# Later heads' queries and keys of the stick-breaking mixer from seven quarter products, their weight sums made by GpSimd

## The reference, cut to what matters

```python
def stick_breaking_mixer(x, w_in, w_out):
    q, k, v = jnp.split(x @ w_in, 3, axis=-1)            # 1024 columns each
    heads = lambda a: a.reshape(B, S, SB_HEADS, HEAD_DIM) # 16 heads of 64
    return stick_breaking_attention(heads(q), heads(k), heads(v)) @ w_out

def one_block(b):                                         # stick_breaking_attention
    z = jnp.einsum('bqhd,bshd->bhqs', qb, k) * scale
    log_1m = jnp.where(mask, jax.nn.log_sigmoid(-z), 0.0)
    between = lax.cumsum(log_1m, axis=3, reverse=True) - log_1m
    w = jnp.where(mask, jnp.exp(jax.nn.log_sigmoid(z) + between), 0.0)
    return jnp.einsum('bhqs,bshd->bqhd', w, v)
```

## Time and profile before

| What | us |
|---|---|
| Median of 3 runs (1143.28 to 1144.44) | 1143.73 |
| The profiled execution | 1144.65 |
| Its span in the trace | 1142.9 |
| PE busy, of the span | 1058.1 |
| DVE busy | 401.9 |
| ACT busy | 221.1 |
| POOL busy (6 instructions) | 1.0 |

### The profile page before, as it was taken

The page is one execution under the profiler, slowest core; times in us unless marked ns, Lnnn a source line. Parts: engine busy times, 40 slices in busy tenths (PEclk is TensorE's granted clock), DMA queues, the critical chain, the costliest instruction groups (busy, mean ns, idle before and its releaser), DMA issues.

```text
span 1142.9 us, 15878 instructions
## 1 busy us (share of the span) xinstructions
PE 1058.1 (93%) x6490; PEld 527.8 (46%) x6490; DVE 401.9 (35%) x1070; ACT 221.1 (19%) x509; POOL 1.0 (0%) x6
## 2 busy tenths in 40 slices
PE   9999999999999999999999999987878897789996
PEld 6555455554786455554655544423222332224231
DVE  5776463114556654114736734101100010001003
ACT  2045341111024432111131522101000000001011
POOL 0000000000000000000000000000000000000000
PEclk9999999999999999999999999999988999899999
DMA  9878478977943378996836738999999999999995
GB/s 320 185 199 292 174 266 357 421 329 251 339 163 132 122 275 346 421 381 208 322 130 228 290 136 290 386 430 425 428 429 426 428 430 427 428 430 428 399 424 231
DMA packets 84997, 363.66 MB, mean 318 GB/s; under 512 B 23138, under 2 KB 28612, under 8 KB 61892
## 3 DMA queue, kind: packets, MB, share of 16 engines
q1 hardware_dynamic: 84132, 362.59, 81.3%
q10 hardware_dynamic: 800, 0.17, 0.1%
HBM read 361.69 MB, written 1.05 MB: 317 GB/s over the span
## 4 chain that ended last, share of the span: by engine, by line
PE 67%; DMA 23%; DVE 6%; ACT 1%; issue 1%; SPq 1%; DVEq 0%
DMA weights<-in_expert_w_down_dram 16%; PE bank L1471 13%; PE bank L1025 6%; PE bank L1003 6%; PE bank L1535 5%; PE bank L1583 5%; DMA weights<-in_expert_w_up_dram 4%; PE bank L1515 4%; PE bank L1684 3%; PE bank L1015 2%; PE bank L1812 2%; PE bank L1403 2%; PE bank L1957 2%; PE bank L1242 2%; DMA weights<-in_expert_w_gate_dram 1%; PE bank L1917 1%
## 5 line engine op out<-in xcount | busy, mean ns | idle before, releaser
L1471 PE MATMUL bank<-weights,mixed 128*32 128x512 f32 x992 | 226.3, 610 | 31.3 <-DMA weights<-in_expert_w_gate_dram 17.9
L1471 PEld LDWEIGHTS bank<-weights,mixed 128*32 128x32 f32 x992 | 63.1, 112 | 181.1 <-issue 169.6
L1025 PE MATMUL bank<-weights,mixed 128*128 128x512 f32 x192 | 89.8, 602 | 0.0
L1003 PE MATMUL bank<-weights,x_transposed 128*128 128x512 f32 x192 | 89.2, 601 | 0.0
L1535 PE MATMUL bank<-weights,work 128*32 128x512 f32 x464 | 62.1, 670 | 25.5 <-DMA weights<-in_expert_w_down_dram 21.0
L3098 DVE TENSOR_TENSOR work<-work,bank 64x512 f32<-64x512 f32 (+1 forms) x22 | 15.0, 682 | 157.7 <-PE bank L1471 156.0
L2285 ACT ACTIVATE work<-bank 128x512 f32<-128x512 f32 (+1 forms) x32 | 19.0, 594 | 229.5 <-PE bank L1535 190.7
L3000 DVE COPY work<-bank 64x512 f32<-64x512 f32 (+1 forms) x30 | 20.7, 690 | 117.0 <-PE bank L1535 75.1
L1684 PE MATMUL bank<-work,heads_transposed 128*128 128x512 f32 x120 | 56.0, 607 | 4.6 <-ACT work L2285 4.6
L1471 PE MATMUL bank<-weights,projected 128*64 128x256 f32 x512 | 57.0, 381 | 0.0
L3005 DVE COPY work<-bank 128x256 f32<-128x256 f32 (+1 forms) x22 | 10.8, 493 | 127.4 <-PE bank L1487 127.4
(11 more groups left out here) (464 smaller groups left out, 1405.8 us busy)
## 6 DMA issues: line engine op xcount, KB each, us to landing
weights<-in_expert_w_gate_dram SPq DMA_DIRECT2D x28, 2048.0 KB, 16.9
weights<-in_expert_w_up_dram SPq DMA_DIRECT2D x28, 2048.0 KB, 17.7
weights<-in_expert_w_down_dram SPq DMA_DIRECT2D x24, 2048.0 KB, 19.1
weights<-in_moe_w_down_dram SPq DMA_DIRECT2D x16, 2048.0 KB, 14.7
weights<-in_moe_w_gate_dram SPq DMA_DIRECT2D x14, 2048.0 KB, 13.0
weights<-in_moe_w_up_dram SPq DMA_DIRECT2D x12, 2048.0 KB, 15.2
weights<-in_sb_w_in_dram SPq DMA_DIRECT2D x6, 2048.0 KB, 19.5
weights<-in_w_in_dram SPq DMA_DIRECT2D x6, 2048.0 KB, 16.2
```

Of the source, the lines that this page charges most:

```text
L1003: i = mm(BANK[bank or 6 + t][:, :], XT[:, kt, t * P:(t + 1) * P], w[:, kt, :], start=kt == 0, stop=kt == KT - 1)
L1025: i = mm(BANK[bank][:, :], mixT[:, kt, t * P:(t + 1) * P], w[:, kt, :], start=kt == 0, stop=kt == KT - 1)
L1471: i = mm(b[n_slots * c:n_slots * (c + 1), e * F:(e + 1) * F], x[:, kt, q * n_slots:(q + 1) * n_slots], extra_weights(c, kt) if outside els ...
```

## The change

Chunks 3 and 4 are no longer projected by eight half-pieces but by seven products (`second`, 16 matmuls of 128 columns each), with the same scheme as the first heads, as fillers of steps 0 to 6. The fillers of chunk 5 move from steps 8, 9 to 7, 8; step 9 has none. GpSimd makes the four sums of weights (`VS1` to `VS4`, 128x2048 each, written into quarters of the chunks' own slots that are no longer read). DVE adds the products up (`sb_sums`, in steps 3, 5, 6 and 7), ACT copies three of them (`sb_copies`, steps 1, 2 and 4). The copy of the last values moves on ACT from step 11 to step 12. The sums of inputs `XS` are kept in `norm_params` instead of `heads_transposed`, and so the load of the second layer's normalisation rows moves from ahead of the mixer's output weights to behind the third chunk of the following experts.

```diff
+        XS = [quarter(NORM_[:, CH * i:CH * (i + 1)]) for i in range(4)]
+        VS1, VS2, VS3, VS4 = K1_HI, Q1_LO, K1_LO, Q1_HI
...
@@ block.gpsimd
+            pool.wait_ge(half_psum, 4)
+            nc.gpsimd.tensor_tensor(VS1, K1_LO, K1_HI, ALU.add).then_inc(pool_filled, 1)
+            pool.wait_ge(half_psum, 5)
+            pool.wait_ge(pool_filled, 2)
+            nc.gpsimd.tensor_tensor(VS3, Q1_LO, K1_LO, ALU.subtract).then_inc(pool_filled, 1)
+            pool.wait_ge(pool_filled, 3)
+            nc.gpsimd.tensor_tensor(VS2, VS1, Q1_LO, ALU.subtract).then_inc(pool_filled, 1)
+            pool.wait_ge(products_psum, AB_PRODUCTS + 3)
+            pool.wait_ge(pool_filled, 4)
+            nc.gpsimd.tensor_tensor(VS4, Q1_HI, VS2, ALU.subtract).then_inc(pool_filled, 1)
@@ block.tensor
-                         (N_SB + 5, 0): (half_copied, 5), (N_SB + 5, 1): (proj_copied, 11)}
+                         (N_SB + 5, 0): (proj_copied, 11), (N_SB + 5, 1): (sums_ready, AB_SUMS + 6)}
...
+            def second_4():
+                second(6, K1_HI, XS[3]).then_inc(half_psum, 1)
+            def second_1():
+                second(7, Q1_LO, lo[:, :, 0:P]).then_inc(half_psum, 1)
+            def second_2():
+                pe.wait_ge(half_copied, 4)
+                second(6, Q1_HI, hi[:, :, 0:P]).then_inc(products_psum, 1)
+            def second_5():
+                pe.wait_ge(half_copied, 5)
+                pe.wait_ge(pool_filled, 2)
+                second(7, VS1, XS[0]).then_inc(products_psum, 1)
+            def second_6():
+                pe.wait_ge(sums_ready, AB_SUMS + 4)
+                pe.wait_ge(pool_filled, 4)
+                second(6, VS2, XS[1]).then_inc(products_psum, 1)
+            def second_7():
+                pe.wait_ge(proj_copied, 10)
+                second(7, VS3, XS[2]).then_inc(products_psum, 1)
+            def second_3():
+                pe.wait_ge(sums_ready, AB_SUMS + 5)
+                pe.wait_ge(pool_filled, 5)
+                second(6, VS4, hi[:, :, P:S]).then_inc(chunk_done, 2)
             sb_filler = {
-                0: lambda: project_half_T(N_SB + 3, 0, 0, 8), 1: lambda: project_half_T(N_SB + 3, 0, 8, 16),
...
-                8: lambda: project_half(N_SB + 5, 0, 0, 4), 9: lambda: project_half(N_SB + 5, 0, 4, 8),
+                0: second_4, 1: second_1, 2: second_2, 3: second_5, 4: second_6, 5: second_7, 6: second_3,
+                7: lambda: project_half(N_SB + 5, 0, 0, 4), 8: lambda: project_half(N_SB + 5, 0, 4, 8),
@@ block.scalar
-            sb_copies = {2: (3, 0), 4: (3, 1), 6: (4, 0), 8: (4, 1), 10: (5, 0), 11: (5, 1)}
+            sb_copies = {1: copy_4, 2: copy_1, 4: copy_5, 10: lambda: take_sb_half(0), 12: lambda: take_sb_half(1)}
@@ block.vector
+            def after_second_2():
+                dve.wait_ge(half_copied, 5)
+                dve.wait_ge(products_psum, AB_PRODUCTS + 3)
+                tt(second_q[:, :, 0:P], four(U2), four(BANK[6]), ALU.add).then_inc(sums_ready, 1)
+            def after_second_6():
+                link(tt(U2, U2, BANK[6], ALU.add))
+                tt(second_q[:, :, P:S], second_q[:, :, P:S], four(U2), ALU.add).then_inc(sums_ready, 1)
+            def after_second_7():
+                link(tt(U2, U2, BANK[7], ALU.add))
+                tt(second_k[:, :, P:S], second_k[:, :, P:S], four(U2), ALU.add)
+                tt(second_k[:, :, 0:P], second_k[:, :, 0:P], four(U2), ALU.add).then_inc(sums_ready, 1)
+            def after_second_3():
+                dve.wait_ge(chunk_done, N_SB + 5)
+                tt(second_q[:, :, P:S], second_q[:, :, P:S], four(BANK[6]), ALU.add).then_inc(proj_copied, 1)
+            sb_sums = {3: after_second_2, 5: after_second_6, 6: after_second_7, 7: after_second_3}
             for s in range(16 + 5):
...
+                if s in sb_sums:
+                    sb_sums[s]()
```

More of the change, by code:

```diff
@@ L142 @@
 OUT_DMAS = 3
-SB_SUMS = 7
-SB_PRODUCTS = 7
+SB_SUMS = 10
+SB_PRODUCTS = 11
 AB_SUMS = 4
@@ L509, in build @@
         WS1, WS2, WS3, WS4 = WK[:, 0:HALF_SLOT], WK[:, HALF_SLOT:SLOT], K_LO, Q_HI
-        XS = [quarter(QK[:, 1024 + CH * i:1024 + CH * (i + 1)]) for i in range(4)]
+        XS = [quarter(NORM_[:, CH * i:CH * (i + 1)]) for i in range(4)]
+        Q1_LO, Q1_HI = (slot(N_SB + 3)[:, at:at + HALF_SLOT] for at in (0, HALF_SLOT))
+        K1_LO, K1_HI = (slot(N_SB + 4)[:, at:at + HALF_SLOT] for at in (0, HALF_SLOT))
+        VS1, VS2, VS3, VS4 = K1_HI, Q1_LO, K1_LO, Q1_HI
         U3, U4, U2 = QK[:, 0:CH], QK[:, CH:2 * CH], QK[:, 6 * CH:7 * CH]
@@ L778, in moe @@
                         load_unit_chunk(0, j)
+                        if L == 1 and j == 2:
+                            load_norm(2, (a["ln_mix_g"][1], a["ln_mix_b"][1]))
                     sp.wait_ge(roped, 7)
@@ L1877, in sb_out_first, with second @@
                     out_part(N_SB + 6, 0, t, 6 + t, range(kt, kt + 1))
-            sb_filler = {
-                0: lambda: project_half_T(N_SB + 3, 0, 0, 8), 1: lambda: project_half_T(N_SB + 3, 0, 8, 16),
-                2: lambda: project_half_T(N_SB + 3, 1, 0, 8), 3: lambda: project_half_T(N_SB + 3, 1, 8, 16),
-                4: lambda: project_half_T(N_SB + 4, 0, 0, 8), 5: lambda: project_half_T(N_SB + 4, 0, 8, 16),
-                6: lambda: project_half_T(N_SB + 4, 1, 0, 8), 7: lambda: project_half_T(N_SB + 4, 1, 8, 16),
-                8: lambda: project_half(N_SB + 5, 0, 0, 4), 9: lambda: project_half(N_SB + 5, 0, 4, 8),
+            def second(bank, weights, x):
+                w = quarter(weights)
+                for c in range(4):
+                    for kt in range(KT // 2):
+                        i = mm(BANK[bank][:, c * P:(c + 1) * P], w[:, kt, c * P:(c + 1) * P], x[:, kt, :],
+                               start=kt == 0, stop=kt == KT // 2 - 1)
+                return i
@@ L2360, in _, with take_sb_half, copy_4, copy_1 @@
             take(6, N_SB, [(t, sbV[:, t, 0:CH], P, CH, 1.0) for t in range(T)])
-            def take_sb_half(c, h):
-                dst = sbV[:, h, CH:2 * CH] if c == 5 else (sbQ, sbK)[c - 3][:, 4 + 2 * h:6 + 2 * h, :]
-                take_half(N_SB + c, h, dst, 1.0, 3 + c - 2)
-            sb_copies = {2: (3, 0), 4: (3, 1), 6: (4, 0), 8: (4, 1), 10: (5, 0), 11: (5, 1)}
+            def take_sb_half(t):
+                take_half(N_SB + 5, t, sbV[:, t, CH:2 * CH], 1.0, 6)
+            four = lambda w: w.rearrange("p (n s) -> p n s", n=4)
+            def copy_4():
+                act.wait_ge(half_psum, 4)
+                ac(sbK[:, 4:8, 0:P], four(BANK[6]), ACT.Copy).then_inc(half_copied, 1)
+            def copy_1():
+                act.wait_ge(half_psum, 5)
+                ac(U2, BANK[7], ACT.Copy).then_inc(half_copied, 1)
+            def copy_5():
+                act.wait_ge(products_psum, AB_PRODUCTS + 4)
+                ac(sbQ[:, 4:8, P:S], four(BANK[7]), ACT.Copy)
+                ac(sbK[:, 4:8, P:S], four(BANK[7]), ACT.Copy).then_inc(proj_copied, 1)
+            sb_copies = {1: copy_4, 2: copy_1, 4: copy_5, 10: lambda: take_sb_half(0), 12: lambda: take_sb_half(1)}
             for s in range(16 + 3):
```

19 lines of the change are left out of this document (12 added, 7 removed).

## The result

The changed kernel takes 1165.88 us (median of 5 runs, 1165.59 to 1167.81), before 1143.73: ratio 1.0198, 95% interval 1.0183 to 1.0213. That is 2.9 us above the range's upper end. The direction was right, the size was not: the rival "turn by instruction" is what happened. The profiled execution, the longest of the five (1167.81 us), has a span of 1166.0 us, before 1142.9.

The account below looks back on a forecast made before the run. The loop over heads was taken as bound by PE, the last layer by its loads. Terms -3.4 + 4.8 + 1.7 + 1.5 + 8.1 = +12.7 gave a median of 1156.4 us; range 1146.0 to 1163.0.

Parts of the forecast that it names:

- turn by instruction: Rival: GpSimd gets its turn after every DVE instruction, delaying head 0 by 10.3 us; +19, 1162.7 us, chance 0.16.
- fewer matmuls: On PE in the loop, seven products of 3.57 us replace eight fillers of 28.4 us: saves 3.4 us.
- the wait behind the last product: At L1017, chunk 5's first filler waits for DVE's add at L3317 to empty bank 6: +4.8 us.
- the clock after it: After the 4.8 us wait PE is granted 0.66 clock for the next 5 us: +1.7 us.
- the last copy a step later: ACT copies the last values in step 12, behind head 12's Abs, Exp, Ln, delaying the first output piece: +1.5 us.
- DVE and GpSimd side by side: GpSimd's sums and DVE's two-operand instructions of heads 0 to 3 disturb each other: +8.1 us including the clock.
- they take turns by head: Main forecast: DVE keeps its turn through a head's five instructions, GpSimd gets its turn during masks; +8.15 us, chance 0.42.
- the far end: Each DVE instruction of a head with two SBUF operands waits for a whole GpSimd sum: +14.4 us.
- no disturbance: Rival: GpSimd's sums and DVE's instructions beside them do not hinder each other; +4.6, 1148.3 us, chance 0.28.
- What costs nothing: ACT's changed copies, DVE's other adds, chunk 4's earlier use and SP's later loads fit into idle time: 0.
- The adds fit into DVE's gaps: Rival: DVE's adds run in its idle time, so L1017 waits under 1.9 us; 1141.8 us with none, chance 0.05.
- The loads hide it: Rival: the last layer's loads start no later, so the end does not move; 1143.7 us, chance 0.05.

Follow-up runs that it names:

- the kernel with DVE's sums: Changed kernel, but DVE makes the four sums, three ahead of the loop; last product's add behind head 7's mask, last copy in step 11: 1143.08 us, ratio 0.9985.
- memsets: Changed kernel with GpSimd's four sums replaced by memsets of the same 128x2048 targets: 1149.75 us, ratio 1.0051.
- copies: Changed kernel with GpSimd's four sums replaced by 128x2048 copies of one operand: 1151.34 us, ratio 1.0061.
- quarters: Changed kernel with each GpSimd sum made as four instructions of 512 columns: 1162.09 us, ratio 1.0155.
- 16 columns: Changed kernel with GpSimd's four sums cut short to 16 of their 2048 columns: 1149.84 us, ratio 1.0049.
- other order: Changed kernel with the last product's add directly behind head 7's mask on DVE, product 7's three adds behind head 6's weight: 1161.23 us, ratio 1.0152.
- the kernels without the long sums: Changed kernel with GpSimd's sums cut to 16 columns, made memsets or one-operand copies, or made by DVE, three ahead of the loop: ratios 1.0049 to 1.0067.

## Why the prediction was wrong, step by step

The terms, predicted and as the loop of the changed kernel's profiled execution shows them, in us:

| step | predicted | measured |
| --- | --- | --- |
| fewer matmuls | -3.4 | -2.6 |
| the wait behind the last product | +4.8 | +4.6 |
| the clock after it | +1.7 | +3.1 |
| the last copy a step later | +1.5 | +1.7 and +1.4 clock |
| DVE and GpSimd side by side | +8.1 | +14.6 |
| sum | +12.7 | +22.8 |

The measured sum is, but for rounding, the 22.9 us by which the loop ends later; the medians differ by 22.15, as the profiled execution was the longest. The -2.6 is from the kernel with DVE's sums; +1.7 is the wait of 2.52 less the 0.80 that stood behind the first output piece before; the last row is 10.40 and 1.72 of wait and 2.5 of slow clock (transposes 0.90 for 0.33, the product 5.50 to its end at 355.11 for 3.6).

*DVE and GpSimd side by side.* The step that failed reads "I take the middle course, in which they take turns by head". There was no row for two engines at once, and the two ends, 0 and 14.4, were both worked out; the choice between them was not one by the nearest row but a halfway point. The argument against the far end, that the five instructions of a head leave hardly a gap to get in, was wrong: three scans back to back let a whole sum in between each two. As the rival had it, head 0 was to make PE wait 10.3 us and the next product 2.4 for ACT; 10.40 and 1.72 came, and product 6, which by turns of heads was to wait 6.0 us, waited for nothing. This is 6.5 of the 10.1 us that the forecast is short, 0.8 of it in the clock. That rival's own sum, 19.0, is still 3.8 short of 22.8: 3.6 of the clock and 0.8 of the matmuls, less 0.6 by which the waits together came out shorter.

The sign by which the prediction was to be found wrong misled as well: the softplus of head 0 did start during the first sum, which was to mean no disturbance and a time near 1148. A DVE instruction that is held shows in the profile as started and long, 1.98 us in place of 0.56, so its length tells and its start does not.

*The clock.* One row, 0.34 of 5 us, was taken as the price of a wait of 4.8 us and of one of 6. The clock cost 3.1 us after 4.58, 2.5 after head 0's, 1.4 after 2.52, where I had taken 1.7, 1.7 and nothing: 3.6 us in all. What decides it stays open: the same wait at L1017, 4.57 or 4.58 us, was followed by 6.66, 6.22, 6.12, 5.84 or 5.40 us (changed kernel, memsets, copies, quarters, 16 columns), and the same 2.52 at L1039 by 3.40 and 3.75 in two kernels (changed, other order) and by 1.95 or 1.96 in the others that have it. The wait's length alone doesn't tell.

*Fewer matmuls.* The mechanism was right, the size 0.8 too large: 3.57 was read from seven products in a row, while those in the loop alternate with scores and transposes and take 3.57 to 3.77 from their start to the start of what follows.

*The wait behind the last product* was right, 4.58 for 4.8, and so was its cause, since moving the add took it to 0.5. *The last copy* was right in its wait. *GpSimd's sum* was 4.5 and not 4.2 us. The GPSIMD Engine Reference of the Trainium skill (3.1, Elementwise) gives 4497 ns for it, and the trace agrees (4.49 to 4.65 us). The bound of 5.2 us up to which undisturbed sums were to be harmless doesn't follow from the times beside it, 327.1 to 340.9 for three sums, which give 4.6; nothing hung on it, as PE waits for GpSimd in no run's list of waits. *What costs nothing* held where head 0 was not late: no wait for the chunk's loads or for ACT's copies of products shows in the kernel with the short sums. Of the rivals, "no disturbance" (1148.3) is what the kernels without the long sums show, 1.0049 to 1.0067 of before, 5.6 to 7.7 us against the 4.6 forecast. "The adds fit into DVE's gaps" did not happen as written. Its condition, a wait under 1.9 us at L1017, was too easy: with 0.52 the kernel is even with before (1.0004) and not below, which fits matmuls that save 0.8 less than it counted; only with the copy back in step 11 besides is it faster (0.9985 and 0.9983). "The loads hide it" is refuted for a loop that ends later (22.9 us of it, 23.1 at the end), and for one that ends earlier as far as 1 to 2 us can be told.

## What to carry to other kernels

Before work goes to GpSimd, list what DVE runs beside it by operands: here each instruction with two SBUF operands that met a GpSimd instruction already reading SBUF was held to its end, even between two of its own kind, and those with an operand in a bank were not. So place such GpSimd work where DVE empties banks, or give it to DVE's idle time. Price a new wait with the slower clock behind it as a range, and follow a delayed engine to everything queued behind the late instruction, not to the first waiter only.

## What the runs showed of the hardware

- One DVE instruction per GpSimd sum: scans of 0.42 us each took 4.61 beside sums of 4.5, and 1.38 beside quarters. GpSimd's whole sums lost next to nothing by it: they took 4.49 to 4.65 us in the loop, 4.53 to 4.62 ahead of it. A quarter lost a little: the first three, before DVE's scans, took 3.74 us together, the last, beside a scan, 1.37.
- A held DVE instruction shows as started and long, not as waiting: the softplus 1.98 us in place of 0.56.
- A wait of 2.52 us left a granted clock of 0.66 in the stretch from 400 to 405 us of the changed kernel, in which it ended, and no loss with the short sums (L1039 1.96 us).
- GpSimd on 128x2048: memset 1.80 us, copy 1.90 to 2.10, sum of two operands 4.5. A quarter of the sum is not a quarter of the time: sixteen quarters took 22.3 us (327.30 to 349.55, DVE's instructions between them), four whole sums 18.5.
